# Six modulation groups moved into three norms, and 768 columns split into two halves, in a two-model transformer kernel

## The reference

```python
for i in range(2):
    mod_l = silu(c)     @ ada_w[i] + ada_b[i]     # 6 parts of 1024: sh1, s1, g1, sh2, s2, g2
    mod_c = silu(c_ctx) @ ada_w[i] + ada_b[i]
    h = rms_norm(x, norm1_g[i]) * (1 + s1) + sh1
    x = x + g1 * mixer(h)                          # i = 0: gated linear attention, i = 1: neighbourhood attention
    h = rms_norm(x, norm2_g[i]) * (1 + s2) + sh2
    x = x + g2 * conv_ffn(h)                       # i = 0: latent and context tokens, i = 1: latent only

def conv_ffn(h):                                   # hidden width 2816
    a, val = split(h @ w_in)
    a = a[t-1] * cw0 + a[t] * cw1 + a[t+1] * cw2 + cb     # along the tokens, context and latent apart
    return (silu(a) * val) @ w_out
```

## Time and profile before

| | |
|---|---|
| time, median of 3 (lowest, highest) | 3794.46 us (3791.37, 3798.23) |
| the profiled execution: time, span | 3800.76 us, 3799.0 us |
| mean granted PE clock | 0.990 |
| busy: PE, PEld, DVE, ACT, POOL | 98%, 79%, 43%, 37%, 6% |
| DMA read over the span | 327.35 MB, 87 GB/s |

### The profile page before, as it was taken

One profiled execution on the slowest core, in us unless ns is written; L12 is line 12 of the kernel. 1 busy time (PEld: TensorE's weight loads), 2 busy tenths in 40 slices (PEclk: granted clock), 3 DMA queues, 4 the chain that ended last, 5 costly groups with the idle time before them and its releaser, 6 DMA issues.

```text
span 3799.0 us, 45595 instructions
## 1 busy us (share of the span) xinstructions
PE 3704.2 (98%) x19204; PEld 2997.4 (79%) x19204; DVE 1622.2 (43%) x2573; ACT 1393.1 (37%) x2270; POOL 241.2 (6%) x197
## 2 busy tenths in 40 slices
PE   8998899999999999999999999999999999999998
PEld 6888878888887977888766778888886677888887
DVE  3217735423434155545564443333336444343333
ACT  3135533212224165323446442342325644234231
POOL 0000010000000001000100001110100000112011
PEclk8999999999999999999999999999999999999999
DMA  6320123343312222333321223323222122332322
GB/s 233 111 84 2 45 67 106 104 135 119 115 59 83 67 67 76 92 98 97 95 63 45 72 73 96 108 89 100 94 94 63 45 73 75 96 107 92 98 95 82
DMA packets 108701, 333.98 MB, mean 88 GB/s; under 512 B 11472, under 2 KB 26704, under 8 KB 108368
## 3 DMA queue, kind: packets, MB, share of 16 engines
q1 hardware_dynamic: 108496, 331.06, 27.6%
HBM read 327.35 MB, written 2.10 MB: 87 GB/s over the span
## 4 chain that ended last, share of the span: by engine, by line
PE 93%; DVE 3%; ACT 3%; DMA 1%; issue 1%; POOL 0%; SPq 0%; DVEq 0%; ACTq 0%
PE ps L638 69%; PE ps L691 6%; PE ps L674 2%; PE ps L739 1%; PE ps L1250 1%; PE ps L1090 1%; PE ps L919 1%; PE ps L1078 1%; PE ps L1069 1%; PE ps L851 1%; PE ps L892 1%; PE ps L1253 1%; PE ps L1294 1%; DMA aw<-ada_d 1%; PE ps L1308 1%
## 5 line engine op out<-in xcount | busy, mean ns | idle before, releaser
L2193 DVE TENSOR_TENSOR wlo<-raw,whi 128x1024 fp32r<-128x1024 f32 (+3 forms) x547 | 621.5, 1138 | 846.9 <-ACT whi L1414 846.4
L1414 ACT ACTIVATE whi<-raw 128x1024 fp32r<-128x1024 f32 (+3 forms) x547 | 526.2, 964 | 787.5 <-PE ps L638 617.9
L638 PE MATMUL ps<-bh,whi 128*128 128x512 f32 x1248 | 496.3, 398 | 0.1
L638 PE MATMUL ps<-bh,wlo 128*128 128x512 f32 x1248 | 486.5, 390 | 0.5 <-DVE wlo L2193 0.5
L638 PE MATMUL ps<-bl,whi 128*128 128x512 f32 x1248 | 486.3, 390 | 0.0
L638 PE MATMUL ps<-ah,whi 128*128 128x512 f32 (+2 forms) x1424 | 423.3, 356 | 0.2 <-ACT gv L1567 0.2
L638 PE MATMUL ps<-al,whi 128*128 128x512 f32 (+2 forms) x1424 | 417.7, 352 | 0.0
L638 PE MATMUL ps<-ah,wlo 128*128 128x512 f32 (+2 forms) x1424 | 415.0, 350 | 0.0
L638 PEld LDWEIGHTS ps<-bh,whi 128*128 128x128 f32 x1248 | 234.6, 188 | 58.9 <-issue 8.1
L638 PEld LDWEIGHTS ps<-ah,whi 128*128 128x128 f32 x1424 | 240.0, 188 | 51.1 <-issue 17.9
L638 PEld LDWEIGHTS ps<-bl,whi 128*128 128x128 f32 x1248 | 234.7, 188 | 50.8 <-issue 3.4
(11 more groups left out here) (394 smaller groups left out, 5969.6 us busy)
## 6 DMA issues: line engine op xcount, KB each, us to landing
raw<-weights_d SPq DMA_DIRECT2D x447, 512.0 KB, 3.5
aw<-ada_d SPq DMA_DIRECT2D x96, 512.0 KB, 3.7
raw<-weights_d SPq DMA_DIRECT2D x48, 256.0 KB, 2.6
raw<-weights_d SPq DMA_DIRECT2D x44, 192.0 KB, 2.3
x<-nab_d SPq DMA_DIRECT2D x24, 256.0 KB, 2.8
x<-x_t_d SPq DMA_DIRECT2D x4, 1024.0 KB, 5.5
dt<-rtab_d SPq DMA_DIRECT2D x16, 256.0 KB, 2.8
out_d<-x SPq DMA_DIRECT2D x4, 512.0 KB, 3.1
```

What stands on the lines that cost most here:

```text
L638: m = e.matmul(p[:, 0:n], tiles(w, i)[:, k, :], xs[:, x0 + k, c0:c0 + n], start=pi == 0 and k == 0 and ti == 0, stop=i == job and k == kt ...
L1414: e.activation(flat(WHI, j), raw(j), ACT.Copy).then_inc(q.did("hi", j))
L2193: e.tensor_tensor(flat(WLO, j), raw(j), flat(WHI, j).bitcast(F32), ALU.subtract).then_inc(q.did("lo", j))
```

## The change

1. Six groups leave `FILL_FFN`: (0,10) and (0,11) go into gap 0, (1,8) and (1,9) into gap 1, (1,10) and (1,11) into gap 2. In each gap PE runs the 8 chunks of two groups into banks 4 and 5 after the sums of squares and ahead of `lin_pair`, and the two turns after it. DVE copies the two groups' rows after the norm's last k-tile, and adds the two biases after it has split the weights of the pair and of the chunk that follows.
2. Each gap has 8 slots for its loads (512 KB each, 4 KB a partition), in memory that is free by then. SP issues the loads of gaps 1 and 2 in one place of its order each, those of gap 0 as seven and one.
3. The other eight groups stay in `FILL_FFN`, and end within the first half of the hidden layer. The columns that `norm2` of block 1 needs (`scale_cols(1, 1)`) are made behind gap 1's biases, no longer at the end of the first `conv_ffn`.
4. `gla_w_out` and the first `conv_ffn` take `HALF` in place of `SEGS`. What reads the products follows: three pieces (384 latent; 128 latent; 256 context) where x or `fpad` is written, two of 384 where the halves need not be told apart.

```diff
-FILL_FFN = [(0, 10), (0, 11)] + [(1, cg) for cg in range(12)]
+FILL_FFN = [(1, cg) for cg in range(8)]
+FILL_GAP = [[(0, 10), (0, 11)], [(1, 8), (1, 9)], [(1, 10), (1, 11)]]
...
+    BOTH_OUTS = [[(0, 0, TC), (TC, TC, 128)], [(0, 384, 384)]]
+    LAT_OUTS = [[(0, TC, TL)]]
...
+        def ada_gap(n):
+
+            for (i, cg), b in zip(FILL_GAP[n], (4, 5)):
+                for g in range(4):
+                    ada_chunk(i, cg, g, b)
+
+        def ada_gap_turns(n):
+            for (i, cg), b in zip(FILL_GAP[n], (4, 5)):
+                ada_turn(i, cg, b)
...
             else:
-                lin("gla_w_out", Y, y_ready, SEGS)
+                lin("gla_w_out", Y, y_ready, HALF)
...
+            ada_gap(2 if i else 0)
             q.note(f"end_fnorm{i}", "pe")
...
                         lin_pair(["ffn_w_in", "ffn_w_in"], H, ready, segs)
+                        ada_gap_turns(2 if i else 0)
...
-        conv_ffn(0, SEGS, iter(()), ada_beside(FILL_FFN))
+        conv_ffn(0, HALF, iter(()), ada_beside(FILL_FFN))
 
 
 
         q.note("end_ffn0", "pe")
+        ada_gap(1)
         q.note("end_nnorm", "pe")
         lr = lambda k: [("nl", "nl", k)]
         lin_pair(["na_w_qkv", "na_w_qkv"], H, lr, [SEGL])
+        ada_gap_turns(1)
...
+            ada_gap_rows(2 if i else 0)
             q.note(f"end_fnorm{i}", "dve")
...
                         following = chunk("ffn_w_in")
+                        ada_gap_adds(2 if i else 0)
                         gate_in(ia, n)
...
+        def add_pieces(S, ct, i, part, c, outs, *ready):
+
+            for r in range(2):
+                for si, pieces in reversed(list(enumerate(outs))):
+                    for b0, c0, n in pieces:
+                        if (c0 < TC) == r:
+                            x = X[:, ct, c0:c0 + n]
+                            q.wait_ge(("mm", c), ("mod", i, 2 * part + 1), *ready[r:r + 1])
...
+            first_in = {SIDE_IN: fence("end_norm0"), SIDE_GAP0: [("gom", 3, 1, 1)], SIDE_GAP0 + 7: [("mm", CORE + 7)],
+                        SIDE_FFN: [("amm", SIDE_GAP0 + 6)], SIDE_FFN + 1: [("amm", SIDE_GAP0 + 7)],
+                        SIDE_GAP1: [("mm", LAST_IN)], SIDE_GAP1 + 3: [("fl", 0, 21, 1)],
+                        SIDE_GAP1 + 6: [("amm", SIDE_GAP1 - 1)], SIDE_GAP2: [("av", 31)]}
...
+            if m >= SIDE_GAP2:
+                return first("na_w_out") + 4
+            if m >= SIDE_GAP1:
+                return LAST_IN + 6
```

More of the change, by code:

```diff
@@ L995, in gla_out @@
             if ct < 2:
-                lin_part(ahead[ct], Y, y_ready, SEGS, 6, 8)
+                lin_part(ahead[ct], Y, y_ready, HALF, 6, 8)
             else:
-                lin("gla_w_out", Y, y_ready, SEGS)
+                lin("gla_w_out", Y, y_ready, HALF)
         with_stats("gla", gla_out, True)
@@ L1719, in gate_in @@
             def gate_in(ia, n):
+                for si, pieces in enumerate(outs):
+                    q.wait_ge(("mm", ia), ("pad", i, n) if n < 2 else ("cv", i, n - 2, len(segs) - 1))
+                    for b0, c0, w in pieces:
+                        o = padded(c0)
+                        e.activation(PADS[n % 2][:, o:o + w], PS[plan[ia][6][si]][:, b0:b0 + w], ACT.Copy
+                                     ).then_inc(q.did("ev", ia, si))
                 for si, (c0, w) in enumerate(segs):
-                    o = 1 if c0 == 0 else 259
-                    q.wait_ge(("mm", ia), ("pad", i, n) if n < 2 else ("cv", i, n - 2, len(segs) - 1))
-                    e.activation(PADS[n % 2][:, o:o + w], PS[plan[ia][6][si]][:, 0:w], ACT.Copy).then_inc(q.did("ev", ia, si))
                     c = CC[n % 2][:, c0:c0 + w]
@@ L1729, in value_in @@
             def value_in(iv, n):
-                for si, (c0, w) in enumerate(segs):
+                for si, pieces in enumerate(outs):
+                    c0, w = pieces[0][1], sum(w for _, _, w in pieces)
                     q.wait_ge(("ev", iv, si), *(fb if n < 11 else [("fhalf", i)]))
@@ L1760, in conv_ffn @@
                         out_ct(ct)
-        conv_ffn(0, SEGS, "gla", iter(()), iter(()))
+        conv_ffn(0, SEGS, BOTH_OUTS, "gla", iter(()), iter(()))
         q.note("end_ffn0", "act")
@@ L2263, in ada_beside, with ada_gap_rows, ada_gap_adds @@
             yield
+        def ada_gap_rows(n):
+            for (i, cg), b in zip(FILL_GAP[n], (4, 5)):
+                ada_rows(i, cg, b)
+        def ada_gap_adds(n):
+            for (i, cg), b in zip(FILL_GAP[n], (4, 5)):
+                ada_add(i, cg, b)
         def beside(side, n=1):
@@ L2484, in dve_program @@
         q.wait_ge(*fence("end_gla"))
+        def add_pieces(S, ct, i, part, c, outs, *ready):
[5 more added lines that the diff above has]
+                            q.wait_ge(("mm", c), ("mod", i, 2 * part + 1), *ready[r:r + 1])
+                            e.scalar_tensor_tensor(x, PS[plan[c][6][si]][:, b0:b0 + n], mod(i, part, r, ct), x, ALU.mult, ALU.add
+                                                   ).then_inc(q.did("ev", c, si))
+                            q.note("x", S, ct, r)
         def add_res(S, ct, i, part, psi, c0, n, ev, *ready, perm=False):
@@ L2544, in value_in @@
             def value_in(iv, n):
-                for si, (c0, w) in enumerate(segs):
+                for si, pieces in enumerate(outs):
+                    c0, w = pieces[0][1], sum(w for _, _, w in pieces)
                     c = CC[n % 2][:, c0:c0 + w]
-                    q.wait_ge(("mm", iv), ("cs", i, n, si))
+                    q.wait_ge(("mm", iv), *[("cs", i, n, s) for s in range(len(segs))])
                     e.tensor_tensor(c, c, PS[plan[iv][6][si]][:, 0:w], ALU.mult).then_inc(q.did("ev", iv, si))
@@ L2570, in conv_ffn @@
                     c = chunk("ffn_w_out")
-                    for si, (c0, w) in enumerate(segs):
-                        add_res(f"ffn{i}" if half else f"ffnh{i}", ct, i, 5, PS[plan[c][6][si]], c0, w, ("ev", c, si))
+                    add_pieces(f"ffn{i}" if half else f"ffnh{i}", ct, i, 5, c, outs)
                     if half:
@@ L2584, in conv_ffn @@
                 scale_cols(1, 0)
-                scale_cols(1, 1)
-        conv_ffn(0, SEGS, "gla", iter(()), ada_beside(FILL_FFN))
+        conv_ffn(0, SEGS, BOTH_OUTS, "gla", iter(()), ada_beside(FILL_FFN))
         q.note("end_ffn0", "dve")
@@ L2611, in dve_program @@
         chunk("na_w_qkv")
+        ada_gap_adds(1)
+        scale_cols(1, 1)
         n_norm(1)
@@ L3165, in weights @@
                     return
-        def first(name):
-            return next(i for i, c in enumerate(plan) if c[0] == name)
         load(lat4(X, 0), XT[:, 0:4, :], "x_lat", 0)
```

86 lines of the change are left out of this document (52 added, 34 removed).

## The result

The changed kernel takes 3771.24 us (median of 5, 3769.14 to 3772.32) against 3794.46 for the kernel before (median of 5 in this comparison, 3791.37 to 3801.54). The ratio is 0.9932, 95% interval 0.9921 to 0.9942. That is 23.2 us less by the medians and 25.8 by the ratio; 25.7 less, 3768.8 us, was the forecast, in a range of 3762 to 3776. The profiled execution took 3770.46, against 3800.76 before: 30.3 less. In it PE is as full as before, and the same number of matmuls is there (compare).

The account below looks back on a forecast made before the run. PE, busy for 98% of the span, was taken to bound the kernel. Its stream's -27.4 with +2.0, +0.8 and -1.1 for gaps 0, 1 and 2 made -25.7: 3768.8 us from the median, range 3762 to 3776.

Parts of the forecast that it names:

- `ffn_w_in`, second half: First conv_ffn, second half of the hidden layer: without modulations, 22 chunks at 8.32 take 183.0, not 203.0: -20.0 us.
- wait for the last value chunk's banks: Behind the second half's ffn_w_in: PE's wait for banks freed by DVE's two multiplications changes with halves: -0.2 us.
- products, first half: First conv_ffn, eight products with ffn_w_out: fewer modulation chunks and no slower 512/256 pairs, 105.5 to 101.1: -4.4 us.
- `ffn_w_in`, first half: First conv_ffn, first half: all 20 modulation chunks stay, halves bring 8.64 to 8.55 a chunk: -1.9 us.
- `gla_w_out`, last products: gla_w_out and the first conv_ffn's last products: some chunks leave the slower pace: -0.9 us, bounds 0 and -3.8.
- gap 0: Gap 0: later norm +0.2, faster clock over the pair -1.3, new wait for DVE's biases +3.1: +2.0 us.
- gap 1: Gap 1: chunks fit the idle time, the full clock gives nothing, the turns cost 0.9 to 1.0: +0.8 us.
- gap 2: Gap 2: eight chunks end late, +0.8; the clock holds over the pair, -2.8; turns +0.9: together -1.1 us.
- The rule that I had set against the part: The halves: by the skill page's gap rule 512 + 256 and 384 + 384 cost alike; this part's sum 4.6 us smaller.
- The later norm: Gap 0: DVE writes x in three pieces, not two, so the last product's latent part and the norm come 0.2 us later.
- my two bounds: Gap 0's pair: the clock, if it holds or not, gains 2.1 or about 0.4 us; 1.3 was taken.
- that rival: na_w_out: nine loads in gap 2 delay its weights and PE starves; 14 us slower, 3808, at 80 GB/s; chance 0.04.

Follow-up runs that it names:

- gaps_only: The changed kernel with 512 and 256 columns again in gla_w_out and the first conv_ffn; 3780.59 us against 3795.61 for the kernel before, ratio 0.9961.
- turns_67: The changed kernel with gap 0's two turns writing banks 6 and 7 instead of 4 and 5; 3766.70 us against 3795.61 for the kernel before, ratio 0.9922.
- adds_early: The changed kernel with gap 0's two biases added on DVE behind the first split of weights; 3770.13 us against 3795.61 for the kernel before, ratio 0.9933.
- half_only: The kernel before with the 384 and 384 halves alone, all fourteen groups still in FILL_FFN; 3791.18 us against 3795.61, ratio 0.9989.

## Why the prediction was right, point by point

The forecast's mechanism and its size hold for the stream, which is the bulk of it. Between the attention of the first block and the chunk behind gap 2 the two profiled executions differ by 25.3; the sum was 25.7. That the sum is so close is partly luck: gap 2 came out 0.9 better, gaps 0 and 1 together 0.9 worse.

| step | forecast | measured |
|---|---|---|
| `ffn_w_in`, second half | -20.0 | -20.03 |
| wait for the last value chunk's banks | -0.2 | -0.06 |
| products, first half | -4.4 | -4.21 |
| `ffn_w_in`, first half | -1.9 | -1.84 |
| `gla_w_out`, last products | -0.9 | -1.0 |
| gap 0 | +2.0 | +2.5 |
| gap 1 | +0.8 | +1.2 |
| gap 2 | -1.1 | -2.0 |

*The stream.* Every term is within 0.2. But one sentence behind them was wrong: that a clean chunk of 512 and 256 columns costs 8.33, as the earlier trace rows showed for `gla_w_out`, and that halves pay beside modulations only. gaps_only has clean chunks of 8.48. The sum didn't suffer, because it priced the second half by the halves' own pace, which is the same everywhere; how it divides between the two parts was mis-sized. The halves are worth 3.65 in the second half of the changed kernel, and I had given them nothing there. Two workings are off by little: 20 x 0.09 is 1.8 and not 1.9, and 12 chunks at 12.4 / 16 are 9.3; the 9.6 comes out only with the four turns priced apart. The rule that I had set against the part (the Trainium skill, "TensorE: Matmul & The Clock Gate", section "Back-to-back issue gap", by which both splits cost alike) holds at the fast pace, 8.32 for either split, and not at the slow one, 8.48. The section gives that rule for single matmuls and says that in a stream the weight loads set the spacing too, which my prediction left out.

*Gap 0.* The later norm was +0.03 and not +0.2. The eight chunks took 3.66 and not 4.6, so PE was idle for 2.4 and not 1.6 us before the pair, and the clock held even so. The pair won 1.97, nearly all that the low clock had cost, where I had taken 1.3 as a middle of 2.1 and 0.4. The wait is as forecast, turns and wait 3.07 against 3.1, and for its reason: turns_67 and adds_early take it away by bank and by order. What I missed is the step after it: behind the 2.1 us of idle time the clock falls again, and the next chunk takes 9.82 in place of 8.41, +1.40. So the clock gives 0.57 in all and not 1.3; it lies within my two bounds, but for a reason that I didn't have.

*Gap 1.* The turns are 0.81, where 0.9 to 1.0 were forecast. The pair is also 0.37 longer (14.01 against 13.64 from its first matmul to the turns). The norm sets its end in both kernels, 1.5 ahead of it, and DVE's `al` take 1.27 to 1.35 from the second on, where the second to fourth of before, beside the low clock, took 1.16 to 1.18. half_only, the other execution with the low clock there, has 1.17 and 1.16 beside it; the twelve with the full clock have none below 1.19 from the second on. No run tests whether the clock is the cause.

*Gap 2.* 64 matmuls of modulations take 3.66 and not 4.6, so the pair isn't late at all: +0.8 was wrong by all of it. I had priced a chunk by its 0.57 in the stream; eight in a row take 0.46 each. The clock (-2.8) is as forecast, the turns are 0.8 and not 0.9.

*Loads.* No L760 in the gaps or beside the first `conv_ffn` waits for a DMA, and `na_w_out` runs in steps of 0.227 from matmul to matmul up to the sums; that rival is out.

*Outside the change.* The profiled execution is 30.3 shorter, 5.0 of it where the change has nothing: 3.5 in the attention of the first block and 1.4 between gap 2 and the second block's first product. Executions of one and the same kernel differ so: turns_67 has the long attention once and the short one once. The changed kernel's two medians, 23.2 and 24.7 less, and its two ratios, 25.8 and 25.4 less, agree with the 25.3 of the stages without these.

## What to carry to other kernels

Moving small work from a stream that is full to a pause that is there anyway pays twice, if the clock would fall behind that pause. Look for what the moved work holds on to behind the pause (here two banks until DVE came round), since the wait of 2.1 us cost 3.6 here, 1.3 of it by the clock. Price matmuls from a stream in the same shapes and the same order, and check a "clean" rate at more than one place: two shapes that agree in one stage may have a second pace in another. Where single executions differ by chance in other stages, read a small change in its own stage, from start to start.
